# Latent attention: angles in an earlier layer, all scores before the softmax, softmax by half and token block

## The reference

```python
def mla_mixer(x, positions, w_in, q_norm_g, kv_norm_g, w_uq, w_ukv, w_out):
    c_q, c_kv, k_rope = jnp.split(x @ w_in, [MLA_Q_RANK, MLA_Q_RANK + MLA_KV_RANK], axis=-1)   # 384, 256, 64
    q = (rms_norm(c_q, q_norm_g) @ w_uq).reshape(B, S, MLA_HEADS, MLA_NOPE + MLA_ROPE)         # 8 heads, 128 + 64
    q_nope, q_rope = jnp.split(q, [MLA_NOPE], axis=-1)
    q_rope = rotary(q_rope, positions)
    kv = (rms_norm(c_kv, kv_norm_g) @ w_ukv).reshape(B, S, MLA_HEADS, MLA_NOPE + MLA_VDIM)
    k_nope, v = jnp.split(kv, [MLA_NOPE], axis=-1)
    k_rope = rotary(k_rope[:, :, None, :], positions)[:, :, 0, :]
    ...
        s = jnp.einsum('bqhd,bkhd->bhqk', qn, k_nope) + jnp.einsum('bqhd,bkd->bhqk', qr, k_rope)
        p = jax.nn.softmax(s.astype(jnp.float32) * scale, axis=-1).astype(v.dtype)
        return jnp.einsum('bhqk,bkhd->bqhd', p, v)
    ...
    return o @ w_out
```

## Time and profile before

| | us |
|---|---|
| median of 3 executions | 3002.99 (2996.99 to 3004.98) |
| the profiled execution | 3003.37 |
| its span | 3001.6 |
| TensorE busy | 2597.4 (87%) |
| VectorE busy | 2282.8 (76%) |
| ScalarE busy | 874.9 (29%) |

### The profile page before, as it was taken

The page is one execution under the profiler, slowest core; times in us unless marked ns, Lnnn a source line. Parts: engine busy times, 40 slices in busy tenths (PEclk is TensorE's granted clock), DMA queues, the critical chain, the costliest instruction groups (busy, mean ns, idle before and its releaser), DMA issues.

```text
span 3001.6 us, 42198 instructions
## 1 busy us (share of the span) xinstructions
PE 2597.4 (87%) x16904; PEld 2319.8 (77%) x16904; DVE 2282.8 (76%) x3225; ACT 874.9 (29%) x1292; POOL 266.1 (9%) x100
## 2 busy tenths in 40 slices
PE   6979999999999996689999999999875674595898
...
PEclk8999999999999997689999999999996555697999
...
GB/s 183 179 84 134 203 210 186 191 179 189 244 256 241 243 208 103 32 92 207 210 190 179 191 179 252 255 241 242 181 148 60 1 15 0 81 154 42 148 171 145
DMA packets 201186, 484.00 MB, mean 161 GB/s; under 512 B 23392, under 2 KB 93408, under 8 KB 200480
## 3 DMA queue, kind: packets, MB, share of 16 engines
...
## 4 chain that ended last, share of the span: by engine, by line
PE 58%; DVE 32%; POOL 4%; issue 2%; DMA 2%; ACT 1%; ACTq 0%; DVEq 0%
PE psum L865 23%; PE psum L662 19%; DVE rounded L1251 7%; DVE halves L2021 7%; PE psum L818 6%; DVE halves L2018 5%; POOL rounded L630 4%; PE psum L1040 2%; DVE rounded L1247 2%; DMA sb<-in_u_turned 1%; DVE sb L1764 1%; PE psum L704 1%; PE psum L943 1%; DVE sb L1286 1%; PE psum L941 1%
## 5 line engine op out<-in xcount | busy, mean ns | idle before, releaser
L1251 DVE TENSOR_TENSOR rounded<-sb,rounded 128x1024 fp32r<-128x1024 f32 (+3 forms) x696 | 813.9, 1172 | 243.0 <-ACT rounded L2242 233.4
L662 PE MATMUL psum<-rounded 128*128 128x256 f32 (+1 forms) x4380 | 728.8, 330 | 84.4 <-DVE rounded L1251 42.3
L818 PE MATMUL psum<-rounded 128*128 128x256 f32 x6144 | 774.2, 285 | 12.6 <-POOL rounded L630 12.4
L662 PEld LDWEIGHTS psum<-rounded 128*128 128x128 f32 x4380 | 655.6, 198 | 157.8 <-DVE rounded L1251 38.8
L2242 ACT ACTIVATE rounded<-sb 128x1024 fp32r<-128x1024 f32 x512 | 542.8, 1060 | 788.5 <-PE psum L818 346.6
L818 PEld LDWEIGHTS psum<-rounded 128*128 128x128 f32 x6144 | 748.1, 192 | 15.2 <-POOL rounded L630 15.2
L865 PE MATMUL psum<-rounded,weights 128*128 128x512 f32 x3072 | 697.3, 389 | 0.4 <-ACT sb L2258 0.4
L865 PEld LDWEIGHTS psum<-rounded,weights 128*128 128x128 f32 x3072 | 576.4, 188 | 120.6 <-issue 1.2
L630 POOL TENSOR_TENSOR rounded<-sb,rounded 128x1024 fp32r<-128x1024 f32 x96 | 265.9, 2785 | 1255.8 <-ACT rounded L2242 1255.3
L1247 DVE CAST rounded<-sb 128x1024 fp32r<-128x1024 f32 (+4 forms) x317 | 192.9, 609 | 134.5 <-PE psum L662 110.0
L2021 DVE TENSOR_TENSOR halves<-halves,small 128x1536 bf16<-128x1536 bf16 x128 | 225.0, 1758 | 4.4
...
## 6 DMA issues: line engine op xcount, KB each, us to landing
sb<-in_u_turned SPq DMA_DIRECT2D x256, 512.0 KB, 3.8
sb<-in_peer_v SPq DMA_DIRECT2D x256, 512.0 KB, 3.6
hidden<-sb SPq DMA_DIRECT2D x256, 128.0 KB, 3.8
sb<-hidden SPq DMA_DIRECT2D x256, 128.0 KB, 3.5
...
```

Source lines behind the costliest of these rows:

```text
L662: mm = pe.matmul(o, a[p], b[q], start=(first and i == 0), stop=(last and i == 2), skip_group_check=True)
L818: mm = pe.matmul(ps(bank, 1)[:, 0:T], u[p][:, k * P:(k + 1) * P], hT[:, q, k, :], start=(k == 0 and w == 0), stop=(k == KD - 1 and w == 2))
L1251: vec.tensor_tensor(ring_lo[0:k, part, 0:wide], ring[0:k, slot, 0:wide], ring_hi[0:k, part, 0:wide].bitcast(F32), ALU.subtract).then_inc(c ...
```

## The change

It has four parts.

1. The cosine and sine of the latent attention are made in peer0. Their buffers and the frequencies and positions move to memory (`early`) that holds the expert layer's routes until its gates are placed. The two parameter loads join those of peer0. VectorE runs the same 17 instructions (`mla_angles`) in turn 192 of the passes, between the split of down tile 67 and its gate weights; ScalarE takes the two sines in turn 194; VectorE waits for them in turn 200.
2. The head of the attention: ScalarE squares the latents straight from PSUM and sums them in the same instruction (four: two blocks, two norms). VectorE copies only the 64 rotary columns a block and scales the latents from PSUM. The wait for the parameters stands ahead of the reciprocal.
3. All scores come first, the first four heads into banks 0 to 3, the others into 4 to 7; TensorE signals after each token block. VectorE takes the maximum of a block's four heads and scales it to a bias; ScalarE takes the exponential of each head out of PSUM with that bias and sums it in the same instruction (16 in all); VectorE takes the reciprocal and scales each head. Half one's transposes go to banks 0 to 3, half two's to 4 to 7, both ahead of the products with V. `p` and `pT` exist twice.
4. The output panel is fed by half: chunks 0 to 3 wait for the first product's split, chunks 4 to 7 for the second's.

```diff
+ANGLES_AT = 128 + 64
...
-                a["p"], a["pT"] = m.take(TB, 4, T), m.take(4, TB, T)
+                a["p"], a["pT"] = [m.take(TB, 4, T) for _ in range(2)], [m.take(4, TB, T) for _ in range(2)]
...
-                a["cos"], a["sin"], a["ang"], a["turn"] = (m.take(TB, ROPE // 2) for _ in range(4))
-                a["freq"], a["posi"], a["pos"] = m.take(ROPE // 2), m.take(TB), m.take(TB)
+                early = Memory(sb, pair_at + 3328, 704)
+                a["cos"], a["sin"], a["ang"], a["turn"] = (early.take(TB, ROPE // 2) for _ in range(4))
+                a["freq"], a["posi"], a["pos"] = early.take(ROPE // 2), early.take(TB), early.take(TB)
...
-                param(phase, a["freq"], x["c_mla_freq"])
-                param(phase, a["posi"].bitcast(I32), x["positions_cols"])
+                param("peer0", a["freq"], x["c_mla_freq"])
+                param("peer0", a["posi"].bitcast(I32), x["positions_cols"])
...
                 for n in range(2):
-                    hold(range(4))
+                    hold(range(4 * n, 4 * n + 4))
                     for tb in range(TB):
                         for i in range(4):
                             hd = 4 * n + i
-                            o = ps(2 * tb + i // 2, 1)[:, (i % 2) * T:(i % 2 + 1) * T]
+                            o = ps(4 * n + 2 * tb + i // 2, 1)[:, (i % 2) * T:(i % 2 + 1) * T]
...
-                    mm.then_inc(psum_for_vec, 1)
-                    pe.wait_ge(*banks.lend(range(4), "v"))
-                    hold(range(4, 8))
-                    wait_all(turn_p(a["p"], 4))
-                    hold([0, 1])
+                        mm.then_inc(psum_for_vec, 1)
+                back = []
+                for n in range(2):
+                    pe.wait_ge(vec_for_pe, to_pe.up(TB))
+                    back.append(turn_p(a["p"][n], 4 * n))
+                for n in range(2):
+                    wait_all(back[n])
+                    hold([2 * n, 2 * n + 1])
                     for i in range(4):
                         for kb in range(TB):
-                            mm = pe.matmul(ps(i // 2, 1)[:, (i % 2) * T:(i % 2 + 1) * T],
-                                           a["v"][:, kb, (4 * n + i) * VDIM:(4 * n + i + 1) * VDIM], a["pT"][:, i, kb, :],
+                            mm = pe.matmul(ps(2 * n + i // 2, 1)[:, (i % 2) * T:(i % 2 + 1) * T],
+                                           a["v"][:, kb, (4 * n + i) * VDIM:(4 * n + i + 1) * VDIM], a["pT"][n][:, i, kb, :],
                                            start=(i % 2 == 0 and kb == 0), stop=(kb == 1), skip_group_check=True)
                     mm.then_inc(psum_for_vec, 1)
-                    o_ready = banks.lend([0, 1], "v")
-                pe.wait_ge(*o_ready)
+                    banks.lend([2 * n, 2 * n + 1], "v")
                 hold(range(4, 8))
-                panel("mla_out", hk, "tokens", 4, D)
+                panel("mla_out", hk, "tokens", 4, D, fed=0)
                 banks.lend(range(4, 8), "v")
...
-                vec.wait_ge(params_loaded, loads[phase])
...
-                vec.tensor_copy(a["turn"], a["ang"]).then_inc(*own.mark(vec_for_act))
-
                 panel_done("mla_in")
                 c, r = a["c"], rstd[:, 0:4]
-                vec.tensor_copy(c, ps(4, 4).rearrange("p (b c) -> p b c", b=TB)[:, :, 0:MLA_IN]).then_inc(*own.next())
-                done()
-                vec.tensor_tensor(a["sq"], c[:, :, 0:Q_RANK + KV_RANK], c[:, :, 0:Q_RANK + KV_RANK], ALU.mult).then_inc(*own.next())
...
-                vec.tensor_reduce(r[:, 0:2], a["sq"][:, :, 0:Q_RANK], AX, ALU.add).then_inc(*own.next())
-                vec.tensor_reduce(r[:, 2:4], a["sq"][:, :, Q_RANK:], AX, ALU.add).then_inc(*own.next())
-                done()
+                vec.wait_ge(act_for_vec, from_act.up())
                 vec.tensor_scalar(r[:, 0:2], r[:, 0:2], 1.0 / Q_RANK, LN_EPS, ALU.mult, ALU.add).then_inc(*own.next())
-                vec.wait_ge(act_for_vec, from_act.up())
                 vec.tensor_scalar(r[:, 2:4], r[:, 2:4], 1.0 / KV_RANK, LN_EPS, ALU.mult, ALU.add).then_inc(*own.mark(vec_for_act))
+                raw = ps(4, 4).rearrange("p (b c) -> p b c", b=TB)
+                vec.tensor_copy(c[:, :, Q_RANK + KV_RANK:], raw[:, :, Q_RANK + KV_RANK:MLA_IN]).then_inc(*own.next())
+                vec.wait_ge(params_loaded, loads[phase])
                 vec.wait_ge(act_for_vec, from_act.up())
                 vec.reciprocal(r, r).then_inc(*own.next())
...
                 for tb in range(TB):
                     for i, s in enumerate((slice(0, Q_RANK), slice(Q_RANK, Q_RANK + KV_RANK))):
-                        vec.scalar_tensor_tensor(c[:, tb, s], c[:, tb, s], r[:, 2 * i + tb:2 * i + tb + 1], a["gain"][:, s],
+                        vec.scalar_tensor_tensor(c[:, tb, s], raw[:, tb, s], r[:, 2 * i + tb:2 * i + tb + 1], a["gain"][:, s],
                                                  ALU.mult, ALU.mult).then_inc(*own.next())
...
-                for i in range(2):
+                def tops(n, tb):
+                    top = a["top"][:, n, tb, :]
                     from_psum()
-                    softmax(ps(0, 4).rearrange("p (r k) -> p r k", k=T), a["p"], top8, sum8, served)
-                    take_turned(a["pT"].rearrange("p h k t -> p (h k) t")[:, 0:4, :], 4)
+                    vec.tensor_reduce(top, ps(4 * n + 2 * tb, 2).rearrange("p (h k) -> p h k", h=4), AX, ALU.max).then_inc(*own.next())
+                    done()
+                    vec.tensor_scalar(top, top, -MLA_SCALE, None, ALU.mult).then_inc(*own.mark(vec_for_act))
+
+                def shares(n, tb):
+                    total = a["sum"][:, n, tb, :]
+                    vec.wait_ge(act_for_vec, from_act.up())
+                    vec.reciprocal(total, total).then_inc(*own.next())
+                    done()
+                    for i in range(4):
+                        v = a["p"][n][:, tb, i, :]
+                        vec.tensor_scalar(v, v, total[:, i:i + 1], None, ALU.mult).then_inc(*(own.mark(vec_for_pe) if i == 3 else own.next()))
+
+                tops(0, 0)
+                tops(0, 1)
+                shares(0, 0)
+                shares(0, 1)
+                tops(1, 0)
+                tops(1, 1)
+                take_turned(a["pT"][0].rearrange("p h k t -> p (h k) t")[:, 0:4, :], 0)
+                shares(1, 0)
+                shares(1, 1)
+                take_turned(a["pT"][1].rearrange("p h k t -> p (h k) t")[:, 0:4, :], 4)
+                for n in range(2):
                     from_psum()
-                    take_split(hT[:, 0, 4 * i:4 * i + 4, :], hT[:, 1, 4 * i:4 * i + 4, :], 0, 2)
+                    take_split(hT[:, 0, 4 * n:4 * n + 4, :], hT[:, 1, 4 * n:4 * n + 4, :], 2 * n, 2)
+                    vec.tensor_copy(a["tmp"][:, 0, 0:1], iota[:, 0:1]).then_inc(*own.mark(vec_for_pe))
...
+            def mla_angles(a):
+
+                vec.wait_ge(params_loaded, loads["peer0"])
...
+                reduced(a["cos"], a["ang"], a["turn"], True)
+                reduced(a["sin"], a["ang"], a["turn"], False)
+                vec.tensor_copy(a["turn"], a["ang"]).then_inc(*own.mark(vec_for_act))
...
+                    if i == ANGLES_AT and phase == "peer0":
+                        mla_angles(A["mla"])
+                    if i == ANGLES_AT + 8 and phase == "peer0":
+                        vec.wait_ge(act_for_vec, from_act.up())
...
-                act.wait_ge(vec_for_act, from_vec.up())
-                act.activation(a["cos"], a["cos"], ACT.Sin).then_inc(*own.next())
-                act.activation(a["sin"], a["sin"], ACT.Sin).then_inc(*own.mark(act_for_vec))
+                act.wait_ge(chunks_done, end["mla_in"])
+                for tb in range(TB):
+                    for i, (c0, w) in enumerate(((0, Q_RANK), (Q_RANK, KV_RANK))):
+                        act.activation(a["sq"][:, tb, c0:c0 + w], ps(4 + 2 * tb, 2)[:, c0:c0 + w], ACT.Square,
+                                       accum_out=rstd[:, 2 * i + tb:2 * i + tb + 1]).then_inc(
+                            *(own.mark(act_for_vec) if tb and i else own.next()))
...
                 for n in range(2):
-                    in_place(rows8(a["p"]), ACT.Exp, scale=MLA_SCALE)
-                    turned_p(a["pT"], 6)
+                    for tb in range(TB):
+                        act.wait_ge(vec_for_act, from_vec.up())
+                        for i in range(4):
+                            act.activation(a["p"][n][:, tb, i, :], ps(4 * n + 2 * tb + i // 2, 1)[:, (i % 2) * T:(i % 2 + 1) * T], ACT.Exp,
+                                           scale=MLA_SCALE, bias=a["top"][:, n, tb, i:i + 1], accum_out=a["sum"][:, n, tb, i:i + 1]
+                                           ).then_inc(*(own.mark(act_for_vec) if i == 3 else own.next()))
+                for n in range(2):
+                    turned_p(a["pT"][n], 4 * n + 2)
...
+                    if i == ANGLES_AT + 2 and phase == "peer0":
```

(4 more changed lines are left out.)

14 lines of the change are left out of this document (6 added, 8 removed).

## The result

The changed kernel took 2964.34 us (median of 4, 2960.04 to 2970.02), the kernel before 3002.59 beside it (4, 2996.99 to 3004.98): a ratio of 0.9876 [0.9854, 0.9899], 38 us. The forecast was 2961, between 2950 and 2974. The profiled execution took 2966.0 with a span of 2964.2, against 3001.6.

The account below looks back on a forecast made before the run. In the latent attention no two engines work at once, so what leaves the chain leaves the time. Terms: 13.0 + 28.5 + 1.7 - 1.2 = 42.0 us off 3003.4 gives 2961.4, forecast 2961, range 2950 to 2974.

Parts of the forecast that it names:

- Opening: Head of the latent attention: the reciprocal runs at 1156.8 instead of 1169.85 us, released by the parameters, gain 13.0.
- The bound, 10: Opening's lower gain, 10 us, if two weight loads beside the gains each hold them up by about 1.5 us.
- Scores to panel: First score to output panel: half one's softmax runs behind half two's scores, F + 52.2 instead of F + 80.7, gain 28.5.
- S + 5.7: Forecast start of half two's transposes, 5.7 us after S, the end of all scores, itself 35.4 after the first score.
- First chunk: Output panel's first chunk: the panel follows the products without a gap, at their clock, gain 1.7, between 0 and 1.7.
- Angles: First expert layer's down pass: 3.84 us of angles against 2.7 spare, TensorE waits once, cost 1.2, between 0 and 3.8.
- Sum: All terms together: 13.0 + 28.5 + 1.7 - 1.2 = 42.0 us gained, from 3003.4 to 2961.4.
- The clock rival: Half clock outlasts the scores, full only in the output panel, so products take 6.0 us more: 2969.7 us, chance 0.14.
- Late gains: Attention's head: the gains' load lands late beside the weight loads, 3 us lost, 2964.4 us, chance 0.10.
- Scores at full clock: Scores keep the full clock because TensorE idles less ahead: 20 us instead of 35.4, 2946 us, chance 0.06.
- Slower: Half clock left by the scores holds through the output panel and into peer1's query panels: 3012 us, chance 0.02.
- softmax not hidden: Half one's softmax isn't hidden, VectorE waiting at the second maximum: 11 of the 28.5 us missing, 2972 us, chance 0.03.

Follow-up runs that it names:

- part one alone: The kernel before with only the angles in peer0 and their two parameter loads with peer0's: 2999.19 us, ratio 0.998.
- the splits late: The changed kernel with the two weight splits at the attention's head, and the two weight loads they free, moved behind the key's rotation: 2964.5 us, 0.9866.
- the gains first: The changed kernel with the gains' loads issued ahead of the two parameters of the mixers' norm: 2959.31 us, 0.9848.
- all four edits: The changed kernel with gains loaded before norms, weight splits behind key rotation, angles in two pieces, plain scores before rotated ones per block: 2941.36 us, 0.9805.

## Why the prediction was right, and where it was off

- *Opening, 13.0 forecast, 11.2 measured.* The mechanism held: the reciprocal was released by the last gain, the ScalarE sums were done in time. The step that failed is "two issues of 0.45 and their gaps (0.97 in all) are gone from ahead of the gains", and the value I took for the weight loads, none. The load lands 9.3 to 9.6 us after the first issue, with six issues or four; the weights beside it add 1.2 more (the runs with part one alone and with the splits late). The bound, 10, held. TensorE's gap there was 12.5 us, not 10.5. I had read the 6.76 of the earlier trace rows as this load's own duration, when a good part of such a time is what is queued ahead: with the gains first it is 5.1, the weight loads beside it included.
- *Scores to panel, 28.5 forecast, 29.3 measured.* The scores took 35.37 where I had 35.4. The second transposes began at S + 5.8 (S + 5.7), the gap was 2.14 (2). A sum output cost 0.09 an exponential where I took 0.05. From the second transposes to the panel it was 10.2 where I had 11.1: the transposes took 2.2 of it and not 3.7, at the full clock for the most part, and the products 8.0 and not 7.4, since the clock fell for a while. That the stretch came so near is in part luck: with the same code in it the traces have 49.6, 51.4 and 53.6 us where I had 52.2.
- *First chunk, 1.7 forecast, 1.4 measured*, 26.68 against 28.06 to the next transposes.
- *Angles, 1.2 forecast, 1.29 measured.* The spare time of 2.7 us from the earlier trace rows was right, and nothing behind it was late.
- *Sum, 42.0 forecast;* 11.2 + 29.3 + 1.4 - 1.3 + 0.2 = 40.8 in these stretches, 37.4 in the spans, 38.3 in the medians. The rest is the 3.4 us outside the attention in this one pair of profiled executions, to which I put no cause.
- *The clock rival.* It asked that the clock not return until the panel. It did return as the first transposes ended, at 0.50 in the stretch of 1239 and 1.00 at 1241; by what the Trainium skill says of transposes (TensorE: Matmul & The Clock Gate, Part 4: PE-mode transpose) it would not have, and here the trace disagrees, as before. But I had not seen the second half of that rival, that it falls again behind the gap: the two products ran partly at half clock, 8.39 against the 7.07 of the kernel with all four edits, for 1.3 us.
- *Late gains* were given 0.10 and are the rival that came nearest, at 1.2 us of its 3; the forecast's own range covered it. *Scores at full clock* had 0.06 and didn't come, but the reason that I gave (TensorE idle less ahead of them) wasn't shown to govern it: in no trace did the clock return while the rows changed with every score matmul. I had written down the 1.15 of a pair as a given, read from the earlier trace rows. That was right for this change and missed the larger one.
- *Slower, and softmax not hidden:* nothing of either; the first half's softmax ran from 1209 to 1223, inside the scores.
